# A two-block kernel whose first adaptive-modulation sums move partly to TensorE, with ScalarE issuing the first loads

## What is computed

```python
c_act = jax.nn.silu(c)                                   # c: (1, 2048)
mod = c_act @ w_ada[l] + b_ada[l]                        # w_ada: (2048, 6*2048)
sh_m, sc_m, gt_m, sh_f, sc_f, gt_f = jnp.split(mod[:, None, :], N_MOD, axis=-1)
h = rmsnorm(x, pre_mix_norm[l]) * (1.0 + sc_m) + sh_m
proj = h @ w_in[l]                                       # 2048 -> 8208 columns
o_hg = hgrn2_group(proj[..., :HG_COLS], lb_all[l], hg_norm[l])
o_gdn = gdn_group(proj[..., HG_COLS:], ...)
y = jnp.concatenate([o_hg, o_gdn], axis=-1) @ w_out[l]
x = x + gt_m * rmsnorm(y, post_mix_norm[l])
```

## Time and profile before

| | us |
|---|---|
| median of 3 runs (2863.16 to 2867.74) | 2863.45 |
| profiled execution | 2857.05 |
| its span, first to last instruction | 2855.3 |

### The profile page before, as it was taken

The page is one execution under the profiler, slowest core; times in us unless marked ns, Lnnn a source line. Parts: engine busy times, 40 slices in busy tenths (PEclk is TensorE's granted clock), DMA queues, the critical chain, the costliest instruction groups (busy, mean ns, idle before and its releaser), DMA issues.

```text
span 2855.3 us, 35187 instructions
## 1 busy us (share of the span) xinstructions
PE 2702.2 (95%) x12829; PEld 2248.9 (79%) x12829; DVE 1937.6 (68%) x2165; ACT 1261.1 (44%) x1422; POOL 22.7 (1%) x12
## 2 busy tenths in 40 slices
PE   2699999899799999999999999999999999999998
PEld 2577878778688888888877788888888888888886
DVE  6969697887866666666665656555557666666667
ACT  2244262454444444444445554444444444444444
POOL 0000000000000000000000000000000000000000
PEclk7799999999899999999999999999999999999999
DMA  8957765657666666666645445665555555555554
GB/s 314 330 204 242 221 228 193 204 177 253 208 217 206 219 215 205 219 200 220 219 163 169 141 138 189 205 198 192 184 177 191 192 189 188 190 186 189 187 187 155
DMA packets 281266, 578.42 MB, mean 203 GB/s; under 512 B 19642, under 2 KB 20308, under 8 KB 280020
## 3 DMA queue, kind: packets, MB, share of 16 engines
q1 hardware_dynamic: 281172, 577.14, 61.4%
HBM read 574.98 MB, written 2.10 MB: 202 GB/s over the span
## 4 chain that ended last, share of the span: by engine, by line
PE 85%; DVE 7%; DMA 4%; issue 2%; ACT 1%; SPq 1%; ACTq 0%; POOL 0%; DVEq 0%; POOLq 0%
PE bank L443 26%; PE bank L444 26%; PE bank L448 26%; PE bank L697 4%; PE bank L694 3%; DMA early<-in_w_ada 2%; DVE acc L1823 2%; DMA ada_raw<-in_w_ada 2%; DVE w_lo L433 1%; DVE gd_t L2176 1%; DVE acc_w L1823 1%; DVE gd_t L1792 1%; PE bank L1095 0%; SPq L569 0%; DVE at_t L1792 0%
## 5 line engine op out<-in xcount | busy, mean ns | idle before, releaser
L433 DVE TENSOR_TENSOR w_lo<-raw,w_hi 128x1024 fp32r<-128x1024 f32 x880 | 1073.8, 1228 | 634.4 <-ACT w_hi L428 632.9
L428 ACT ACTIVATE w_hi<-raw 128x1024 fp32r<-128x1024 f32 x880 | 930.4, 1059 | 1268.7 <-PE bank L448 1132.1
L443 PE MATMUL bank<-w_hi,op_a_hi 128*128 128x512 f32 x2272 | 906.7, 399 | 38.4 <-DVE op_a_lo L1792 36.7
L444 PE MATMUL bank<-w_hi,op_a_lo 128*128 128x512 f32 x2272 | 892.5, 393 | 0.0
L448 PE MATMUL bank<-w_lo,op_a_hi 128*128 128x512 f32 x2272 | 611.8, 391 | 5.2 <-DVE w_lo L433 5.2
L443 PEld LDWEIGHTS bank<-w_hi,op_a_hi 128*128 128x128 f32 x2272 | 431.6, 190 | 129.1 <-DVE op_a_lo L1792 37.0
L448 PEld LDWEIGHTS bank<-w_lo,op_a_hi 128*128 128x128 f32 x2272 | 429.3, 189 | 96.8 <-DVE w_lo L433 6.2
L444 PEld LDWEIGHTS bank<-w_hi,op_a_lo 128*128 128x128 f32 x2272 | 431.9, 190 | 87.1 <-issue 1.0
L443 PE MATMUL bank<-w_hi,hid_hi 128*128 128x512 f32 x832 | 326.4, 392 | 0.0
L444 PE MATMUL bank<-w_hi,hid_lo 128*128 128x512 f32 x832 | 323.9, 389 | 0.0
L448 PE MATMUL bank<-w_lo,hid_hi 128*128 128x512 f32 x832 | 222.6, 389 | 0.0
(11 more groups left out here) (240 smaller groups left out, 1879.1 us busy)
## 6 DMA issues: line engine op xcount, KB each, us to landing
raw<-in_w_in SPq DMA_DIRECT2D x264, 512.0 KB, 4.7
raw<-in_w_ff SPq DMA_DIRECT2D x256, 512.0 KB, 3.6
raw<-in_ffn_w_up SPq DMA_DIRECT2D x176, 512.0 KB, 3.9
ada_raw<-in_w_ada SPq DMA_DIRECT2D x96, 512.0 KB, 5.3
raw<-in_ffn_w_down SPq DMA_DIRECT2D x88, 512.0 KB, 4.6
early<-in_w_ada SPq DMA_DIRECT2D x30, 1024.0 KB, 12.8
raw<-in_w_out SPq DMA_DIRECT2D x32, 512.0 KB, 4.9
ada_raw_f<-in_w_ada SPq DMA_DIRECT2D x32, 512.0 KB, 4.6
```

Source lines behind the costliest of these rows:

```text
L428: nc.scalar.activation(w_hi[:, gj % RAW], raw[:, j % RAW], ACT.Copy).then_inc(hi_ready, 1)
L433: nc.vector.tensor_tensor(w_lo[:, gj % RAW], raw[:, j % RAW], w_hi[:, gj % RAW].bitcast(F32), ALU.subtract).then_inc(lo_ready, 1)
L443: nc.tensor.matmul(where[:, t], hi(kt + k, tok), w_hi[:, s, k], start=first and k == 0, stop=False)
L444: nc.tensor.matmul(where[:, t], lo(kt + k, tok), w_hi[:, s, k], start=False, stop=False)
```

## The change

ScalarE issues pieces 0 to 3 of the early stage as its first instructions; SyncE starts with piece 4. `ab_raw` is loaded behind piece 13 instead of behind `X`, and ScalarE rounds it after `round_early(1)`. `EARLY_LOADS` places raw pieces 12 and up later among the early pieces. In even turns the fourth row block goes to TensorE (`early_turn`): 8 products of a 128x128 block of `w_ada` itself with a column of `c_act`, added into the PSUM columns in which `early_sums` then adds VectorE's part. So VectorE does 6 instructions in even turns and 8 in odd ones. A buffer is free again when both engines have used it (`early_used`). On TensorE the shares stand ahead of the GEMM loop (turns 0 and 2), behind `early_sums` (turns 4, 8, 12) and behind the fourth step of a group (turns 6, 10, 14). VectorE does turn 0 ahead of `newton(0)`.

```diff
+EARLY_PE = [(3,), ()]
+EARLY_DVE = [[_k for _k in range(4) if _k not in _x] for _x in EARLY_PE]
-EARLY_LOADS = {7: range(0, 4), 11: range(4, 8), 17: (8, 9), 19: (10, 11), 21: (12, 13), 25: (14, 15), 27: (16, 17), 29: (18, 19)}
+EARLY_LOADS = {7: range(0, 4), 11: range(4, 8), 17: (8, 9), 19: (10, 11), 25: (12, 13), 27: (14, 15), 29: (16,), 31: (17, 18, 19)}
+EARLY_ACT = 4
...
+        def early_sums_done(pairs):
+            return 2 * sum(len(EARLY_DVE[p % 2]) for p in range(pairs))
...
-            sp.dma_start(ab_raw[:], w_in[:, HG_COLS + 4096:HG_COLS + 4112].rearrange("(k p) n -> p k n", p=P)) \
-                .then_inc(ab_landed, 16)
             def load_early(n):
                 if n >= EARLY:
-                    sp.wait_ge(ada_used, 4 * (n - EARLY + 2 - n % 2))
+                    sp.wait_ge(ada_used, early_sums_done((n - EARLY) // 2 + 1))
+                    sp.wait_ge(early_used, (n - EARLY) // 4 + 1)
...
-            for n in range(32):
+            for n in range(EARLY_ACT, 32):
                 load_early(n)
+                if n == 13:
+                    sp.dma_start(ab_raw[:], ...).then_inc(ab_landed, 16)
                 for m in EARLY_LOADS.get(n, ()):
                     load_in(m)
...
+            def early_turn(q, r):
+                if r == 0:
+                    pe.wait_ge(*((mod_ready, q - 1) if q >= 2 else (xt_ready, 4)))
+                m = 4 * q + r
+                if not EARLY_PE[m % 2]:
+                    return
+                for x in range(2):
+                    pe.wait_ge(early_landed[(2 * m + x) % EARLY], 16 * ((2 * m + x) // EARLY) + 16)
+                for x in range(2):
+                    src = early_at(2 * m + x)
+                    for k in EARLY_PE[m % 2]:
+                        kt = 4 * r + k
+                        for j in range(4):
+                            mm = nc.tensor.matmul(early_column(q, x, j), src[:, k, j * P:(j + 1) * P], c_act[:, kt:kt + 1],
+                                                  start=r == 0 and k == EARLY_PE[0][0] and x == 0 and j == 0, stop=False)
+                mm.then_inc(early_used, 1)
...
+            for r in range(4):
+                early_turn(0, r)
...
                     if n % 6 == 0:
                         early_sums(n // 6)
+                        if n < 18:
+                            early_turn(n // 6 + 1, 0)
                         pe.wait_ge(op_lo, n // 6 + 1)
...
                     piece(pe, 0, n, hi, lo, PK * k, pair(c), k == 0, k == KP - 1)
+                    if n % 2 and n < 18:
+                        early_turn(n // 6 + 1, (n % 6 + 1) // 2)
...
+            for n in range(EARLY_ACT):
+                nc.scalar.dma_start(early_at(n)[:], early_piece(n)).then_inc(early_landed[n], 16)
             exp_ln_tables()
...
-            act.wait_ge(ab_landed, 16)
-            f(ab_hi[:], ab_raw[:], ACT.Copy, gd["ab_hi"])
...
                 round_early(q)
+                if q == 1:
+                    act.wait_ge(ab_landed, 16)
+                    f(ab_hi[:], ab_raw[:], ACT.Copy, gd["ab_hi"])
...
-                for k in range(4):
+                for k in EARLY_DVE[n % 2]:
...
+            add_early(0)
             newton(0)
             scaled_rows()
-            for n in range(4):
+            for n in range(1, 4):
                 add_early(n)
+            dve.wait_ge(early_used, 2)
             early_split(0, 1, 2, 3)
```

More of the change, by code:

```diff
@@ L351, in two_blocks @@
         ada_used = sem("ada_used")
+        early_used = sem("early_used")
         hi_ready = sem("hi_ready")
@@ L415, in raw_landed, with early_piece @@
             eng.wait_ge(landed[j % RAW], 4 * (s + j - j % RAW) + 16)
+        def early_piece(n):
+            q, r, x = n // 8, n % 8 // 2, n % 2
+            c0 = D * x + CH * q
+            return w_ada[4 * P * r:4 * P * (r + 1), c0:c0 + CH].rearrange("(k p) n -> p k n", p=P)
+        def early_sums_done(pairs):
+            return 2 * sum(len(EARLY_DVE[p % 2]) for p in range(pairs))
         def early_at(n):
@@ L518, in two_blocks @@
         N_LOADED = 16 * (1 + len(row_src) + 3)
-        ADA_BASE = 8 * KT
+        ADA_BASE = 2 * 2 * sum(len(x) for x in EARLY_DVE) * 4
         ADA_COLS = [3 * D, 4 * D, 2 * D, 5 * D]
@@ L575, in load_in @@
                 load(sp, 0, n, win_piece(n))
-            for n in range(32):
+            for n in range(EARLY_ACT, 32):
                 load_early(n)
+                if n == 13:
+                    sp.dma_start(ab_raw[:], w_in[:, HG_COLS + 4096:HG_COLS + 4112].rearrange("(k p) n -> p k n", p=P)) \
+                        .then_inc(ab_landed, 16)
                 for m in EARLY_LOADS.get(n, ()):
@@ L708, in column_sums, with early_column @@
                 tile_done(mm, n, mod_ready, done)
+            def early_column(q, x, j):
+                n = TILE[("mod", 0, f"t{q}")]
+                c = CH * (q % 2) + 4 * x + j
+                return flat(n)[:, c:c + 1]
+            def early_turn(q, r):
[14 more added lines that the diff above has]
+                mm.then_inc(early_used, 1)
             def early_sums(q):
-                pe.wait_ge(ada_used, 32 * (q + 1))
+                pe.wait_ge(ada_used, early_sums_done(4 * (q + 1)))
                 n = TILE[("mod", 0, f"t{q}")]
-                tile_free(n)
                 for x in range(2):
                     for j in range(4):
-                        mm = mul(flat(n)[:, 4 * x + j:4 * x + j + 1], acc[:, x, (4 * q + j) * P:(4 * q + j + 1) * P], ones[:, 0:1])
+                        mm = nc.tensor.matmul(early_column(q, x, j), acc[:, x, (4 * q + j) * P:(4 * q + j + 1) * P], ones[:, 0:1],
+                                              start=False, stop=x == 1 and j == 3)
                 tile_done(mm, n, mod_ready, q + 1)
@@ L1930, in add_early @@
                     dve.wait_ge(early_landed[(2 * n + x) % EARLY], 16 * ((2 * n + x) // EARLY) + 16)
-                for k in range(4):
+                used = early_sums_done(n)
+                for k in EARLY_DVE[n % 2]:
                     kt = 4 * r + k
@@ L1935, in add_early @@
                         if kt:
-                            dve.wait_ge(ada_used, 8 * n + 2 * k + x - 1)
+                            dve.wait_ge(ada_used, used - 1)
                         add_ada(c_act[:, kt:kt + 1], src, dst, kt == 0)
+                        used += 1
             def early_operand(q):
@@ L1943, in early_operand @@
                 part = slice(4 * q, 4 * q + 4)
-                st.mark(tt(shift_m[:, part], flat(n)[:, 0:4], bias[:, part], ALU.add))
-                tt(scale_m[:, part], flat(n)[:, 4:8], bias[:, KT + 4 * q:KT + 4 * q + 4], ALU.add, mod_ready)
+                c = CH * (q % 2)
+                st.mark(tt(shift_m[:, part], flat(n)[:, c:c + 4], bias[:, part], ALU.add))
+                tt(scale_m[:, part], flat(n)[:, c + 4:c + 8], bias[:, KT + 4 * q:KT + 4 * q + 4], ALU.add, mod_ready)
                 dve.wait_ge(mod_ready, q + 1)
```

5 lines of the change are left out of this document (1 added, 4 removed).

## The result

The changed kernel takes 2864.89 us (median of 20 runs), the kernel before 2858.63 (20 runs, among them the three quoted above). The ratio is 1.0020 with a 95% interval of 1.0011 to 1.0028: **3 to 8 us slower**. 2864.89 lies in the range of the forecast, but the forecast was a gain of 0.25 us, with 0.64 on no difference and 0.16 on slower, so its direction was wrong. One of the 20 runs of the changed kernel took 4639.77 us at a granted clock of 0.557; the ratio leaves it out. The profiled execution of the changed kernel has a span of 2860.8 us against 2855.3.

The account below looks back on a forecast made before the run. The moment TensorE begins its fourth group, 160.65 us, was taken to bound the kernel. Terms 20.5 + 27.5 + 48.6 + 6.6 + 31.0 + 26.2 gave 160.4, a gain of 0.25 us: 2863.2 us, range 2856.0 to 2870.0.

Parts of the forecast that it names:

- X's landing: Start of the front: X lands at 20.5 us, range 18.5 to 24.1, against 18.5 in the kernel before.
- The even share: DMA at the start: if ScalarE's and SyncE's queues share the rate evenly, X lands at about 22.5 us.
- piece 7 X + 27.5: Early loads: piece 6 is issued at X + 17.1 us, and piece 7 lands some 10.4 us after that.
- from there to piece 19 48.6: Saturated loads from piece 7's landing to piece 19's: 46.1 us as before, plus 2.5 for ab_raw.
- turn and `low` 6.6: From piece 19's landing to TensorE's second group: VectorE's turn 5.4 us and `op_a_lo` 1.2.
- second to third group 31.0: TensorE's second group to third: 30.4 us plus 0.6 waiting for piece 27, against 34.8 before.
- third to fourth 26.2: TensorE's third group to fourth: 18.0 + 1.95 + 1.95 + 4.3 us, against 25.95 before.
- the prediction's own formula: Whole front: the gain in us is 23.25 - X - a, with X its landing and a the cost of ab_raw.
- the early issue buys nothing, because the buffers and not the issue bound it: ScalarE's issue of pieces 0 to 3: piece 7 lands at 48.0 us, 1.4 later than before.
- ab_raw: 2.5 taken: ab_raw behind piece 13, in the saturated loads: costs 2.5 us, bounds 0.5 and 6.5.
- with VectorE off the path they count: TensorE's shares of turns 6, 10, 14 between GEMM steps: 1.95 us each added to its chain.
- The slower one: Queue ahead of pieces 7 and 14: X 24.1, ab_raw 6.5, gain -7.4 us, 2870.8; slower if X + a exceeds 23.25; chance 0.17.

Follow-up runs that it names:

- the best kernel: Changed kernel without TensorE shares in turns 0 to 3, ab_raw behind all early pieces, two pieces issued by ScalarE: 2843.41 us, 0.9952 of the kernel before.
- the kernel with ab_raw last: Changed kernel without TensorE shares in turns 0 to 3, ab_raw loaded behind all early pieces, four pieces still issued by ScalarE: 0.9968 of the kernel before.

## Why the prediction was wrong

**What bounds.** Right: the moment of the fourth group carried 4.5 of the 5.5 us of span, and landings set the second group.

**X's landing, the term that failed.** The sum took 20.5 and gave 24.1 as its bound; it was 25.85. The step was "if X comes last, 7.6 MB / 0.387": it counted bytes at the full rate and put "the small loads ahead of X may slip too" at nothing, as they "are wanted only for turn 0 and `newton`, which waits for X anyway". They slipped 7.6 us, and X stands behind them on SyncE's queue. The count of bytes was nearly right: at 12 us 2.58 MB of ScalarE's pieces and 1.11 MB of the small loads were through. But the last 0.2 MB are many small packets, and beside ScalarE's they took until 21 us, with the engines at only 230 and 308 GB/s from 16 to 20 us. The even share between X and ScalarE's pieces never came into play: when X's bytes moved, from 18 us on, ScalarE's queue had 0.16 of its 4.19 MB left. The even share that the prediction drew from the Trainium skill ("DMA: Bandwidth & Descriptors", section "Queues, rings and completion order"), X at 22.5, was too early as well. The Trainium skill speaks there of turns by packets and not by bytes, and the trace shows what that can mean: from 8 to 12 us SyncE's queue had 35% of the packets and 10% of the bytes. The Trainium skill's rule in the section "Issuing engines are not separate DMA queues" of the same page, that issuing from several engines only saves sequencer time, fits the gain of the early issue (ScalarE issues at 0.75 us what SyncE issued from 10.1 us on, worth 2.4 us by itself). It says nothing of the price, X's place in time.

**The rest of the sum.** The terms were: piece 7 X + 27.5, measured 25.0 (X at 25.85, the turn at 50.83); from there to piece 19 48.6, measured 51.5 (50.83 to VectorE's turn at 102.29, which waits for it); turn and `low` 6.6, measured 6.6; second to third group 31.0, measured 30.0, of which 0.6 is a wait for piece 27 that did not come (VectorE began turn 13 at 132.29 without one); third to fourth 26.2, measured 26.25. Of the 2.9 us too much up to piece 19, 1.2 are a second dip of the DMA rate behind the restart, and the rest is open:

```profile
50.00:55.00 5.00, 0.00 (x0) 0.00 (x0) 4.17 (x7) 1.88 (x2) 0.00 (x0) 0.50 0.92 294
```

The terms add up to 139.3 behind X against 139.9 forecast. With X at 25.85 the prediction's own formula gives 23.25 - 25.85 - 2.5 = -5.1, that is 5.1 us *slower*, against 4.5 measured on the group and 5.5 on the span.

**The parts.** The step "the early issue buys nothing, because the buffers and not the issue bound it" was right about the gate, and only because of the share of turn 0; without the share the same issue gained 2.4 us. ab_raw: 2.5 taken, 2.5 measured. The new order with the shares: 3.8 us expected between second and third group, 4.8 measured (34.8 to 30.0), and 3.8 by the order alone (31.0). The shares: "with VectorE off the path they count" was right (24.7 us from third to fourth group with the order alone, 26.25 with shares), and all eight alone moved the fourth group by 0.0.

**The rivals.** The slower one (X delayed, ab_raw holing the stretch) had the right place and half the right mechanism: X was late, ab_raw cost no more than the 2.5 forecast. The sign that was named for it, X's squares past 23 us, came (25.9). Its condition, X + a over 23.25, was met by 28.35, its own threshold for 0.2% being 29.0. Its price took X at 24.1, which passed for the worst case. A chance of 0.16 for slower was low for a term that no row of the trace showed.

**The median.** 2863.45 of three runs was high; twenty gave 2858.63. The predicted 2863.2 was near the measured 2864.89 only through that, which is luck: from 2858.63 the same forecast would have been 2858.4.

## What to carry over

Before a second queue is filled early, look for what the first queue still has to bring: bulk transfers beside it hold up small loads, and with them all that stands behind them in their queue. Here the first 2.1 MB cost X 0.6 us and the next 2.1 MB 6.7. When a second engine is made a reader of a rotating buffer, its place in its own program becomes a condition of the next load: put its shares only in turns where it is ready at the same time as the first, and check that they gain anything there (0.5 us here). Two edits that are harmless alone are to be checked for a path that runs through both.

## What the runs showed of the hardware

- 4.2 MB on ScalarE's queue, issued at 0.75 us, moved the landing of the last of the small loads on SyncE's queue from 13.5 to 21.1 us, and 2.1 MB only to 14.2. The delay is far from proportional: the first two pieces cost 0.7 us, the next two 6.9. With two pieces ScalarE's queue was through before 12 us, with four it still moved 0.59 MB from 14 to 16 us.
- A load of 2048 stretches of 64 bytes (0.13 MB) takes 2.5 us of the whole DMA rate out of a saturated queue, where its bytes are worth 0.3.
- A restart of an empty queue: from the issue at 42.80, 27 GB/s in the first window of a microsecond (43 to 44), then 172, then 369.
- The rear, from the fourth group on, took 2690.6 to 2707.0 us in the profiled executions, a spread of 16.4 us, where the best kernel is 13.4 us ahead at the fourth group. Executions of one kernel that take longer show a lower granted clock: of the nine of the kernel with ab_raw last, 2843.45 us at 0.980 and 2856.97 us at 0.976. What moves the clock was not tried.
